# A decoder layer on eight cores: the second core's columns go from one piece to two, on either side of the first core's, and two equal tiles share their instructions

## The chip, the cores and the metric

The kernel runs on all 8 cores of one Trainium2 chip. The input holds four sequences of 4096 positions with 1024 channels; cores 0 and 1 share the first sequence, 2 and 3 the second, and so on. The even core of a pair is the "first core" (role `a` in the code), the odd one the "second core" (role `b`). The pairs do not talk to each other, and neither do the two cores of a pair. The time is that of the slowest core, in microseconds (us) on the device. A TensorE instruction multiplies a 128 x 128 weight block with up to 512 columns; a "column" is one position of the sequence.

## The reference

One layer with two token mixers and a gated channel mixer, cut to what matters:

```
h  = rmsnorm(x)
u_pool, u_rnn, u_gate, g_pool, g_rnn = split(h @ w_in)         # 512 + 4 x 1024 outputs
y_pool = pool_mixer(u_pool) @ w_pool_out                       # trailing windows of 2, 4, 8, 16
v  = conv4(u_rnn)                                              # causal, 4 taps, per channel
r, i = sigmoid(v @ w_a + b_a), sigmoid(v @ w_x + b_x)          # 8 diagonal blocks of 128
a  = exp(-8 * r * softplus(-lam))
hr[t] = a[t] * hr[t-1] + sqrt(1 - a[t]^2) * i[t] * v[t]        # over the whole sequence
y_rnn = (hr * gelu(u_gate)) @ w_rnn_out
x  = x + (sigmoid(g_pool) * y_pool + sigmoid(g_rnn) * y_rnn) @ w_o
x  = x + (silu(rmsnorm(x) @ w_gate) * (rmsnorm(x) @ w_up)) @ w_down   # 2816 inner channels
out = rmsnorm(x)
```

The recurrence `hr` runs over all 4096 positions. A core that gives out columns in the middle or at the end of a sequence must therefore first run the recurrence alone (norm, `u_rnn`, convolution, gates, scan) over every column ahead of them.

## The kernel before, in words

Channels lie on the 128 partitions, positions along the free dimension. Columns 0 to 2239 (`XS = 2240`) are given out by the first core, the other 1856 by the second, which before that runs the recurrence alone over columns 0 to 2239. Such recurrence-only columns are called the prefix. Given-out columns are worked off in two chunks (`own`), and each chunk in tiles of up to 508 columns: 256, 412, 396 and 344, 500, 332 on the first core, 508, 508 and 460, 380 on the second, whose prefix has tiles of 256 and four times 496. A chunk loads all weights of the layer again.

In `chunk`, a given-out column goes through 36 blocks of `w_in` (`wu` recurrence, `wg` its gelu gate, `wq` pool, `wa` and `wb` merge gates), 16 gate blocks `keep_rg`, pool output `keep_wp`, `wr`, `wo`, and then the channel mixer: 22 blocks `wf` (gate and up) and 8 blocks `wz` (down). Counted in matmuls per tile this is 288 + 16 + 32 + 64 + 64 + 352 + 176 = 992; a prefix column needs 64 + 16 = 80. `stat` adds the squares of the channels on TensorE, either with one matmul of a sum made elsewhere or with eight (`"pe"`).

For one head and tile, `rnn_group` has TensorE write `u` into a PSUM bank; ScalarE makes `v` from it (L745) and VectorE adds three taps (L757); GpSimd casts to bf16 (L765); TensorE makes the two gates (L770), ScalarE their tanh (L780) and exp (L788), GpSimd a square (L795), ScalarE a sqrt (L798), VectorE the product and the scan (L815, L828). Instructions from L788 on already cover all tiles of a group.

Nothing of the order is written by hand. `Planner` places every instruction of a role on its engine by a list of keys (the tables in `ROLES`), estimated durations and the space in SBUF and PSUM, and the engines then run that order strictly, with semaphores between them. All weights are issued by GpSimd's DMA queue (`load` with `pool`), all tiles of `x` by SyncE's (`load_tile`). The first instructions (`start`) are common to both roles.

## Time and profile before

| | |
|---|---|
| median of 3 runs (lowest, highest) | 1025.53 us (1024.29, 1219.17) |
| the profiled execution | 1024.35 us |
| its span on the slowest core (core 3, a second core) | 1022.8 us |
| spans of the first cores (0, 2, 4, 6) | 1017.9, 1016.8, 1017.4, 1021.7 us |
| spans of the second cores (1, 3, 5, 7) | 1022.7, 1022.8, 1022.7, 1022.4 us |
| TensorE busy, core 3 / core 2 | 924.4 / 980.4 us |
| mean granted TensorE clock, core 3 / core 2 | 0.951 / 0.986 |

A span runs from the first to the last instruction of a core; the profiled execution's own time is 1.5 us longer than the longest span. PE is TensorE, PEld its weight loads, DVE VectorE, ACT ScalarE, POOL GpSimd, SP SyncE. In a table of stretches the busy time of each engine stands with its number of instructions in brackets, and PEclk is the mean granted clock in that stretch (1.00 is 2.4 GHz, the lower level of 1.2 GHz is 0.50).

### The profile page before, as it was taken

The numbers are of one execution on the slowest core, as the hardware profiler recorded it, in microseconds if no ns is written. First come the engines' busy times: TensorE is split into PE (matmuls) and PEld (weight loads), VectorE is DVE, ScalarE is ACT, GpSimd is POOL, SyncE is SP. The second block draws the span as 40 slices with busy tenths as digits, with TensorE's granted clock in tenths as the row PEclk, the third lists the DMA queues.
The fourth block names the chain that finished last, engine by engine and source line by source line (L and its number), as shares of the span: only waits on it lengthen the run. The fifth ranks groups of instructions, "written<-read, shape, count | busy, mean of one in ns | idle before, by whom it ended". The sixth has DMA issues, their size and how long they took to land.

```text
span 1022.8 us, 13708 instructions; the slowest of 8 cores (1016.8 to 1022.8 us)
## 1 busy us (share of the span) xinstructions
PE 924.4 (90%) x4484; PEld 446.6 (44%) x4484; DVE 591.4 (58%) x798; ACT 556.7 (54%) x804; POOL 336.8 (33%) x347
## 2 busy tenths in 40 slices
PE   2378688698978999999999999999999999999995
PEld 1134233233433444444444444444555555555553
DVE  2179998999999867844253544533644452222235
ACT  2579997989889942548264938611722351111112
POOL 2438593778655641151001122112251211000000
PEclk8579789899989999999999999999999999999998
DMA  8921452003644276768403257255939175910003
GB/s 176 242 69 33 160 93 42 12 1 55 116 82 87 38 192 118 160 98 150 82 8 56 39 80 141 44 101 123 253 69 212 30 129 108 211 41 2 1 1 135
DMA packets 42765, 96.88 MB, mean 95 GB/s; under 512 B 3776, under 2 KB 19264, under 8 KB 42560
## 3 DMA queue, kind: packets, MB, share of 16 engines
q0 software_dynamic: 23904, 63.45, 36.1%
q1 hardware_dynamic: 18784, 32.48, 10.6%
q8 instruction: 40, 0.66, 0.2%
q14 instruction: 37, 0.30, 0.1%
HBM read 151.75 MB, written 7.60 MB: 156 GB/s over the span
## 4 chain that ended last, share of the span: by engine, by line
PE 78%; ACT 9%; issue 5%; POOL 3%; DVE 2%; DMA 2%; ACTq 0%; DVEq 0%; SPq 0%; POOLq 0%
PE bank L705 74%; PE bank L770 2%; PE bank L667 2%; DMA wu<-w_in 2%; ACT th L780 1%; DVE v L757 1%; ACT q L798 1%; POOL sq L638 1%; ACT th L788 1%; ACT v L745 1%; ACT L798 1%; ACT L780 1%; DMA xt<-xT 1%; POOL vb L765 1%; ACT wi L780 0%
## 5 line engine op out<-in xcount | busy, mean ns | idle before, releaser
L705 PE MATMUL bank<-h,wf 128*128 128x508 bf16 (+2 forms) x1408 | 280.7, 358 | 0.0
L705 PEld LDWEIGHTS bank<-h,wf 128*128 128x128 bf16 x1408 | 136.5, 97 | 139.9 <-issue 0.8
L757 DVE SCALAR_TENSOR_TENSOR v<-bank,keep_cst,v 128x496 f32<-128x496 f32 (+3 forms) x200 | 128.8, 683 | 32.4 <-POOL v L754 13.4
L705 PE MATMUL bank<-h,wu 128*128 128x500 bf16 (+4 forms) x576 | 130.1, 381 | 16.3 <-DMA wu<-w_in 11.0
L1084 DVE TENSOR_TENSOR ff<-tf,bank 128x508 bf16<-128x508 f32 (+2 forms) x88 | 55.7, 634 | 147.9 <-PE bank L705 123.5
L705 PE MATMUL bank<-ff,wz 128*128 128x508 bf16 (+2 forms) x704 | 139.5, 359 | 0.0
L1079 ACT ACTIVATE tf<-bank 128x508 f32<-128x508 f32 (+2 forms) x88 | 48.8, 557 | 137.8 <-PE bank L705 134.4
L652 ACT ACTIVATE sq<-x 128x508 f32<-128x508 f32 (+2 forms) x56 | 32.9, 590 | 125.3 <-DVE x L1096 97.4
L705 PEld LDWEIGHTS bank<-ff,wz 128*128 128x128 bf16 x704 | 68.9, 98 | 68.6 <-issue 0.5
L705 PEld LDWEIGHTS bank<-h,wu 128*128 128x128 bf16 x576 | 58.7, 103 | 83.9 <-issue 32.9
L765 POOL CAST vb<-v 128x496 bf16<-128x496 f32 (+3 forms) x68 | 61.1, 905 | 61.4 <-DVE v L757 53.3
L770 PE MATMUL bank<-vb,keep_rg 128*128 128x496 bf16 (+4 forms) x144 | 43.2, 381 | 33.4 <-ACT th L780 10.1
L515 POOL DMA_DIRECT2D wf<-wfi x44 | 23.8, 549 | 147.1 <-PE bank L705 106.0
L795 POOL TENSOR_TENSOR q<-th 128x752 f32<-128x752 f32 (+3 forms) x31 | 56.9, 1843 | 37.8 <-ACT th L788 18.9
L682 DVE SCALAR_TENSOR_TENSOR h<-xt,keep_cst,bank 128x500 bf16<-128x500 f32 (+4 forms) x72 | 45.8, 686 | 30.8 <-ACT bank L674 29.7
L745 ACT ACTIVATE v<-bank,keep_cst 128x496 f32<-128x496 f32 (+3 forms) x72 | 51.7, 732 | 19.1 <-PE bank L705 18.0
L705 PE MATMUL bank<-h,wa 128*128 128x508 bf16 (+2 forms) x256 | 56.6, 367 | 3.0 <-ACT th L780 1.7
L1096 DVE TENSOR_TENSOR x<-bank,x 128x508 f32<-128x508 f32 (+2 forms) x32 | 20.4, 639 | 64.9 <-PE bank L705 64.6
L705 PE MATMUL bank<-h,wg 128*128 128x508 bf16 (+2 forms) x256 | 55.2, 367 | 2.8 <-ACT th L780 1.9
L780 ACT ACTIVATE th<-bank,keep_hb 128x496 f32<-128x496 f32 (+3 forms) x72 | 44.8, 639 | 22.1 <-PE bank L770 21.8
L638 POOL TENSOR_TENSOR sq<-sq,sq 128x1000 f32<-128x1000 f32 (+2 forms) x18 | 41.9, 2330 | 36.9 <-ACT sq L623 30.3
L705 PE MATMUL bank<-h,wb 128*128 128x508 bf16 (+2 forms) x256 | 53.9, 363 | 0.0
(103 smaller groups left out, 1311.7 us busy)
## 6 DMA issues: line engine op xcount, KB each, us to landing
wf<-wfi POOLq DMA_DIRECT2D x44, 512.0 KB, 9.5
wz<-wfo POOLq DMA_DIRECT2D x16, 704.0 KB, 10.1
xt<-xT SPq DMA_DIRECT2D x16, 500.0 KB, 8.6
wu<-w_in POOLq DMA_DIRECT2D x16, 256.0 KB, 13.7
xt<-xT SPq DMA_DIRECT2D x8, 512.0 KB, 21.1
wa<-w_in POOLq DMA_DIRECT2D x16, 256.0 KB, 5.9
wg<-w_in POOLq DMA_DIRECT2D x16, 256.0 KB, 5.4
wb<-w_in POOLq DMA_DIRECT2D x16, 256.0 KB, 5.5
```

The costliest lines, as they stand in the source:

```text
L638: self.ew(adds, 2 * w, key, lambda e, t=t: e.tensor_tensor(out=sq.tensor[:], in0=sq.tensor[:], in1=t.tensor[:], op=ALU.add), [sq, t], [sq] ...
L652: g.op("act", c_act(w), key, lambda e: e.activation(out=s.tensor[:], in_=x2[cc // 2].tensor[:, cc % 2, :], func=AF.Square), rd=[(x2[cc // ...
L682: g.op("dve", c_dve(w) + 0.04, key + 0.1 * kc, lambda e, kc=kc, b=b, o=o, h=h: e.scalar_tensor_tensor(out=o.tensor[:, h, :], in0=b.tensor[ ...
L705: last = e.matmul(p.tensor[:, 0:n], lhsT=wap(kc), rhs=rhs(kc), start=(kc == 0), stop=(kc == K - 1))
L745: g.op("act", c_act(w, 2), k, lambda e, p=p, o=o, w=w: e.activation(out=v.tensor[:, o:o + w], in_=p.tensor[:, HALO:HALO + w], func=AF.Iden ...
L757: g.op("dve", c_dve(w), k, lambda e, p=p, o=o, w=w, s=s: e.scalar_tensor_tensor(out=v.tensor[:, o:o + w], in0=p.tensor[:, HALO - s:HALO - ...
L765: cast = lambda e, vb=vb, o=o, w=w: e.tensor_copy(out=vb.tensor[:], in_=v.tensor[:, o:o + w])
L770: g.op("pe", c_mm(w) + 0.05, k + 1 + 0.3 * q, lambda e, pg=pg, q=q, vb=vb, w=w: e.matmul(pg.tensor[:, 0:w], lhsT=self.rg.tensor[:, q, j, : ...
L780: g.op("act", c_act(w, 1), k + 1 + 0.3 * q, lambda e, pg=pg, out=out, hcol=hcol, w=w: e.activation(out=out(), in_=pg.tensor[:, 0:w], func= ...
L795: g.op("pool", 0.09 + 0.0018 * W, k, lambda e: e.tensor_tensor(out=q2.tensor[:], in0=th.tensor[:], in1=th.tensor[:], op=ALU.mult), rd=allp ...
L1079: g.op("act", c_act(w), kf, lambda e, pg=pg, th=th, w=w: e.activation(out=th.tensor[:], in_=pg.tensor[:, 0:w], func=AF.Silu), rd=[pg], wr= ...
L1084: g.op("dve", c_dve(w), kf, lambda e, pu=pu, th=th, fb=fb, w=w: e.tensor_tensor(out=fb.tensor[:], in0=th.tensor[:], in1=pu.tensor[:, 0:w], ...
```

## The change

The first core now gives out columns 800 to 2923 and the second columns 0 to 799 and 2924 to 4095. Each has a prefix: 800 columns on the first core (tiles 256, 272, 272, ahead of its first chunk, `pre_at=0`), 2124 on the second (424, 424, 416, 428, 432, between its two chunks, `pre_at=1`). The chunks have tiles 508, 508 and 368, 472, 268 on the first core, 256, 272, 272 and 388, 392, 392 on the second. The weights `wu` of the neighbouring chunk are used for the prefix too.

Where two tiles that follow each other have the same width, `rnn_pair` joins them: their `u` and gates go to two neighbouring PSUM banks, and L745, the three L757, L765 and the two L780 are issued once for both. This holds for 272, 272 and 508, 508 on the first core, for 272, 272 and 424, 424 and 392, 392 on the second. A bank pair must be free as a whole (`find_bank`). The gate weights come in four loads, not one. A load of an `x` tile now waits for the weight load that the planner sees end 4 us before it. All tables in `ROLES` are new, so nearly all instructions stand in another order.

```diff
-XS = 2240
+Y0, Y1 = 800, 2924
...
+    def find_bank(self, b, t):
+
+        free = [self.bank_live[i] is None and self.banks[i][0] <= t for i in range(8)]
+        if b.space == "ps2":
+            c = [(max(self.banks[i][0], self.banks[i + 1][0]), i) for i in range(0, 8, 2) if free[i] and free[i + 1]]
+        else:
+            c = [(self.bank_live[i ^ 1] is None, self.banks[i][0], i) for i in range(8) if free[i]]
+        return min(c)[-1] if c else None
...
+        weights = sorted([o for o in self.order["pool"] if o.nbytes], key=lambda o: o.end)
+        for o in self.order["sp"][sum(h.eng == "sp" for h in self.head):]:
+            if o.nbytes and o.tag != "out":
+                begin = o.end - self.prm["dma_lat"] - o.nbytes / self.prm["dma_rate"]
+                t = [x for x in weights if x.end <= begin - 4.0 and x.start < o.start]
+                if t:
+                    o.deps.append(t[-1])
...
+    def rnn_pair(self, j, tiles, wu, key, toff, v, th, wi, cast, off, part):
+        w = tiles[0][1]
+        two = lambda b: b.tensor[:, off:off + 2 * w].rearrange("p (t w) -> p t w", t=2)
+        p = self.banks("ps_u")
...
+        for s in (1, 2, 3):
+            g.op("dve", c_dve(2 * w) + 0.05, k, lambda e, s=s: e.scalar_tensor_tensor(
+                out=two(v), in0=p.tensor[:, :, HALO - s:HALO - s + w],
+                scalar=cst.tensor[:, C_CW + 8 * (3 - s) + j:C_CW + 8 * (3 - s) + j + 1], in1=two(v),
+                op0=ALU.mult, op1=ALU.add), rd=pk + [cst] + vk, wr=vk, tag="cv")
...
+        for ci, widths in enumerate(own):
+            if ci == at:
+                pre, wus, col = self.prefix(col, wus)
+            col, wus = self.chunk(ci, widths, prm["keys"][ci], pre if ci == at else [], wus if ci == at else None, col, ci + 1 == at)
...
-        groups=[], own=[[256, 412, 396], [344, 500, 332]], wp=344.8, window2=183.19,
+        prefix=[256, 272, 272], groups=[1, 2], own=[[508, 508], [368, 472, 268]], wp=268.52, window2=1485.95,
...
-        prefix=[256, 496, 496, 496, 496], groups=[2, 2, 1], own=[[508, 508], [460, 380]], wp=261.84, window2=107.54,
+        prefix=[424, 424, 416, 428, 432], groups=[2, 2, 1], own=[[256, 272, 272], [388, 392, 392]], wp=116.07, window2=8149.02,
```

How the instructions move is shown at three places. In these rows `x2` means the same instruction twice in a row, and `waits d_pool7` names a semaphore of a weight load on GpSimd's queue. The first place is SyncE's queue on the first core, just after the common start; before, it holds the `x` tiles of 416 and 400 columns:

```order
L515 DMA xt_70<-xT 128x2x416
L515 DMA xt_71<-xT 128x2x416
L515 DMA xt_72<-xT 128x2x416
L515 DMA xt_73<-xT 128x2x416
L515 DMA xt_83<-xT 128x2x400
L515 DMA xt_84<-xT 128x2x400
L515 DMA xt_85<-xT 128x2x400
L515 DMA xt_86<-xT 128x2x400
```

and now the second prefix tile (276 with its 4 columns of overlap) and the first chunk's two tiles:

```order
L535 DMA xt_87<-xT 128x2x276 [waits d_pool3]
L535 DMA xt_88<-xT 128x2x276 [waits d_pool4]
L535 DMA xt_89<-xT 128x2x276
L535 DMA xt_90<-xT 128x2x276 [waits d_pool5]
L535 DMA xt_186<-xT 128x2x512 [waits d_pool6]
L535 DMA xt_187<-xT 128x2x512 [waits d_pool7]
L535 DMA xt_188<-xT 128x2x512 [waits d_pool8]
L535 DMA xt_189<-xT 128x2x512 [waits d_pool9]
L535 DMA xt_199<-xT 128x2x512 [waits d_pool10]
L535 DMA xt_200<-xT 128x2x512 [waits s_pe]
L535 DMA xt_201<-xT 128x2x512 [waits d_pool11]
L535 DMA xt_202<-xT 128x2x512 [waits d_pool12,s_dve]
```

The tiles were issued at once; now nearly each waits for one more weight block to land, and there are sixteen of them instead of eight.

The second place is TensorE on the second core, after the first heads of its first tile (`h` the normalised input, `acc` and `sq` sums of squares). Before, recurrence only:

```order
L667 MATMUL bank<-acc_1042,keep_ones_48 128x500
L667 MATMUL bank<-sq_1235,keep_ones_48 128x512
L667 MATMUL bank<-acc_1084,keep_ones_48 128x500
L705 MATMUL bank<-h_1044,wu_59 128x500 x2
L705 MATMUL bank<-h_1045,wu_59 128x500 x2
L705 MATMUL bank<-h_1046,wu_59 128x500 x2
L705 MATMUL bank<-h_1047,wu_59 128x500 x2
L705 MATMUL bank<-h_1044,wu_60 128x500 x2
L705 MATMUL bank<-h_1045,wu_60 128x500 x2
L705 MATMUL bank<-h_1046,wu_60 128x500 x2
L705 MATMUL bank<-h_1047,wu_60 128x500 x2
```

and now:

```order
L729 MATMUL bank<-h_1034,wg_1086 128x256 x2
L729 MATMUL bank<-h_1035,wg_1086 128x256 x2
L729 MATMUL bank<-h_1036,wg_1086 128x256 x2
L729 MATMUL bank<-h_1037,wg_1086 128x256 x2
L729 MATMUL bank<-h_1047,wu_1071 128x276 x2
L729 MATMUL bank<-h_1048,wu_1071 128x276 x2
L729 MATMUL bank<-h_1049,wu_1071 128x276 x2
L729 MATMUL bank<-h_1050,wu_1071 128x276 x2
L729 MATMUL bank<-h_1047,wg_1086 128x272 x2
L729 MATMUL bank<-h_1048,wg_1086 128x272 x2
L729 MATMUL bank<-h_1049,wg_1086 128x272 x2
L729 MATMUL bank<-h_1050,wg_1086 128x272 x2
```

The prefix was all that TensorE had there; now blocks of `wg` (and soon `wb`, `wq`, `wa`) of the first chunk stand between those of `wu`.

The third place is TensorE on the second core in the channel mixer of its first chunk. Before, `wf` follows `wf`:

```order
L667 MATMUL bank<-acc_1427,keep_ones_48 128x508
L705 MATMUL bank<-h_1450,wf_1524 128x508 x2
L705 MATMUL bank<-h_1451,wf_1524 128x508 x2
L705 MATMUL bank<-h_1452,wf_1524 128x508 x2
L705 MATMUL bank<-h_1453,wf_1524 128x508 x2
L705 MATMUL bank<-h_1450,wf_1469 128x508 x2
L705 MATMUL bank<-h_1451,wf_1469 128x508 x2
```

and now:

```order
L729 MATMUL bank<-h_1299,wf_1374 128x256 x2
L729 MATMUL bank<-h_1300,wf_1374 128x256 x2
L729 MATMUL bank<-h_1510,wu_57 128x428 x2
L729 MATMUL bank<-h_1511,wu_57 128x428 x2
L729 MATMUL bank<-h_1512,wu_57 128x428 x2
L729 MATMUL bank<-h_1513,wu_57 128x428 x2
L691 MATMUL bank<-acc_1550,keep_ones_48 128x432
L729 MATMUL bank<-h_1524,wu_57 128x428 x2
L729 MATMUL bank<-h_1525,wu_57 128x428 x2
L729 MATMUL bank<-h_1526,wu_57 128x428 x2
L729 MATMUL bank<-h_1527,wu_57 128x428 x2
L729 MATMUL bank<-h_1307,wf_1360 128x272 x2
```

The whole prefix (`wu` with 420 to 436 columns and the gates) has moved into and behind this stage, between the `wf` blocks of 256 and 272 columns.

## Rows read from the trace of the kernel before

**Rows 1.** Span and mean granted TensorE clock, core by core.

```profile
core 2: 1016.8 us, clock 0.986
core 3: 1022.8 us, clock 0.951
```

**Rows 2.** Chain that ended last, by engine: core 3, then core 2.

```profile
PE 78%; ACT 9%; issue 5%; POOL 3%; DVE 2%; DMA 2%; ACTq 0%; DVEq 0%; SPq 0%; POOLq 0%
...
PE 92%; DMA 2%; DVE 2%; issue 2%; ACT 1%; POOL 0%; SPq 0%; DVEq 0%; ACTq 0%; POOLq 0%
```

**Rows 3.** Busy times by stretch, core 3; the first line names the columns.

```profile
core 3: us, PE busy (x) PEld busy (x) DVE busy (x) ACT busy (x) POOL busy (x), PEclk, DMA share, GB/s
0.00:75.00 75.00, 34.51 (x113) 17.30 (x114) 26.91 (x54) 37.04 (x53) 26.24 (x30) 0.70 0.70 166
75.00:426.00 351.00, 303.63 (x1318) 130.72 (x1317) 315.94 (x359) 277.39 (x393) 209.54 (x170) 0.93 0.41 84
426.00:1000.00 574.00, 574.00 (x2985) 291.57 (x2984) 235.08 (x363) 238.91 (x355) 101.02 (x148) 1.00 0.48 90
1000.00:1023.00 23.00, 12.23 (x73) 6.99 (x71) 13.43 (x24) 3.40 (x7) 0.00 (x0) 0.82 0.43 150
```

**Rows 4.** The same for core 2, first its first 75 us.

```profile
0.00:75.00 75.00, 52.85 (x252) 31.87 (x253) 34.03 (x72) 40.72 (x70) 21.22 (x43) 0.89 0.89 169
...
0.00:243.00 243.00, 218.65 (x1336) 138.47 (x1338) 159.75 (x233) 143.91 (x256) 100.04 (x122) 0.96 0.59 115
243.00:1000.00 757.00, 757.00 (x4675) 457.30 (x4673) 361.08 (x569) 300.97 (x490) 114.60 (x158) 1.00 0.42 83
1000.00:1017.00 17.00, 4.74 (x30) 2.82 (x28) 5.87 (x12) 1.95 (x4) 0.00 (x0) 0.77 0.25 84
```

**Rows 5.** Timeline (start, us, engine): first up-and-gate matmuls, core 2, then core 3.

```profile
243.22 1.91 PE L705 MATMUL bank<-h,wf 128*128 128x256 bf16 x16
...
425.83 5.32 PE L705 MATMUL bank<-h,wf 128*128 128x508 bf16 x24
```

**Rows 6.** Waits of TensorE on core 3: us in total, times, longest.

```profile
PE bank L705 <- DMA wu<-w_in: 11.0, 2, 6.2
...
PE bank L770 <- DVE v L757: 8.5, 5, 4.2
```

**Rows 7.** Matmuls of core 2 by form: count, busy us, mean ns.

```profile
L705 PE MATMUL bank<-h,wf 128*128 128x500 bf16 x352 | 77.8, 373 | 0.0
...
L705 PE MATMUL bank<-h,wf 128*128 128x256 bf16 x352 | 41.3, 272 | 0.0
...
L667 PE MATMUL bank<-sq,keep_ones 128*128 128x416 f32 x16 | 6.2, 522 | 2.0 <-ACT sq L623 2.0
```

**Rows 8.** The statistics matmuls of core 3 by form.

```profile
L667 PE MATMUL bank<-sq,keep_ones 128*128 128x512 f32 x32 | 16.6, 627 | 7.6 <-ACT sq L623 7.5
...
L667 PE MATMUL bank<-sq,keep_ones 128*128 128x260 f32 x16 | 5.3, 505 | 7.9 <-ACT sq L623 7.9
```

**Rows 9.** VectorE on core 3 by form.

```profile
L757 DVE SCALAR_TENSOR_TENSOR v<-bank,keep_cst,v 128x508 f32<-128x508 f32 x48 | 33.0, 734 | 1.4 <-ACT v L745 0.8
...
L1084 DVE TENSOR_TENSOR ff<-tf,bank 128x380 bf16<-128x380 f32 x22 | 12.1, 550 | 39.9 <-PE bank L705 38.4 <-ACT sq L652 1.5
...
L757 DVE SCALAR_TENSOR_TENSOR v<-bank,keep_cst,v 128x256 f32<-128x256 f32 x24 | 11.1, 475 | 12.7 <-ACT v L745 6.3 <-ACT ab L582 5.6
```

**Rows 10.** ScalarE on core 3 by form.

```profile
L798 ACT ACT_TABLE_LOAD x27 | 34.6, 1283 | 1.6 <-POOL q L795 1.1
...
L1079 ACT ACTIVATE tf<-bank 128x380 f32<-128x380 f32 x22 | 10.7, 487 | 45.9 <-PE bank L705 45.9
```

**Rows 11.** Timeline of ScalarE on core 3 around one table load.

```profile
28.71 1.28 ACT L780 ACT_TABLE_LOAD   x1
30.00 0.47 ACT L780 ACTIVATE th<-bank,keep_hb 128x256 f32<-128x256 f32 x1
```

**Rows 12.** Timeline of core 3: the last writes of x.

```profile
1015.67 4.25 DVE L682 SCALAR_TENSOR_TENSOR x<-x,keep_cst,bank 128x380 f32<-128x380 f32 x8 [2.38 <-ACT bank L674]
```

More of the change, by code:

```diff
@@ L164, in can_alloc @@
                 continue
-            if b.space == "ps":
-                if not any(self.bank_live[i] is None and self.banks[i][0] <= t for i in range(8)):
+            if b.space != "sb":
+                if self.find_bank(b, t) is None:
                     return False
@@ L169, in can_alloc @@
                 n += b.nbytes
-        if room and any(b.space == "ps" and b.left is not None for b in o.bufs):
+        if room and any(b.space != "sb" and b.left is not None for b in o.bufs):
             room = 0
@@ L737, in rnn_group @@
         off = 0
+        joined = 0
         for i, (h, w, part) in enumerate(tiles):
+            if joined:
+                joined = 0
+                continue
+            if i + 1 < len(tiles) and tiles[i + 1][1] == w and not (ps or on[2] or on[5]):
+                self.rnn_pair(j, tiles[i:i + 2], wu, key + toff * i, toff, v, th, wi, kk_vb, off, i)
+                joined = 1
+                off += 2 * w
+                continue
             k = key + toff * i
@@ L962, in chunk @@
+        i = 0
+        for gi, n in enumerate(prm["groups"]):
+            base, step, toff = P["rnn"][gi]
+            self.rnn_groups(P["bat"], [(
+                j, [(h, w, None) for h, w in pre[i:i + n]], wus[j], base + step * j + P["off"][gi][j], toff, first and gi == 0, None,
+                self.places(P, j), gi == len(prm["groups"]) - 1) for j in range(8)])
+            i += n
+        return pre, wus, col
+    def chunk(self, ci, widths, kk, pre, wus, col, parted):
         g, dr, prm = self.g, self.dr, self.prm
@@ L979, in chunk @@
         tw = list(zip(hs, widths))
-        first = self.role == "a" and ci == 0
+        first = col == 0
         G = []
```

201 lines of the change are left out of this document (117 added, 84 removed).

## Prediction

> **What bounds the kernel now.** I read the spans first: second and first cores end close together, at 1022.8 and 1016.8 us, but with different clocks [rows 1]. The chain that ended last says why: TensorE is 78% of it on core 3 and 92% on core 2 [rows 2]. So a first core is a TensorE queue with a late start, and a second core is something else in front of one. The stretches show where. Core 2 has TensorE busy for all of 243 to 1000 us at full clock [rows 4]. Core 3 reaches that state only at 426 us; from 75 to 426 us TensorE works 303.6 of 351 us at a mean clock of 0.93 while VectorE is busy 315.9 us [rows 3]: there the recurrence of 2240 prefix columns plus the first chunk keeps VectorE (90%) and ScalarE (79%) as the limit, and TensorE goes idle and, when idle, slow.
>
> I split each span into **work** (TensorE's busy time times its granted clock, what it would take at 2.4 GHz) and **loss** (the rest). Core 3: 34.5 x 0.70 + 303.6 x 0.93 + 574.0 + 12.2 x 0.82 = 890.6 of work, 132.2 of loss: 51 before 75 us, 69 up to 426, 13 in the tail [rows 3]. Core 2: 218.7 x 0.96 + 757.0 + 4.7 x 0.77 = 970.5 of work, 46.3 of loss: 33 up to its first `wf` matmul at 243 us and 13 in the tail [rows 4, 5]. A clock averaged over a stretch is not quite that of its busy time, so these are good to some 3 us.
>
> **The change part by part.** *Columns.* A given-out column is 992 matmul columns and a prefix column 80. First core: 2240 x 992 = 2,222,080 becomes 2124 x 992 + 800 x 80 = 2,171,008, or 51,072 fewer. Second core: 1856 x 992 + 2240 x 80 = 2,020,352 becomes 1972 x 992 + 2124 x 80 = 2,126,144, or 105,792 more. The price is the slope between `wf` matmuls of 500 and 256 columns, 77.8/352 = 221.0 ns and 41.3/352 = 117.3 ns [rows 7]: 0.425 ns a column. That is -21.7 us and +45.0 us, on the path everywhere.
>
> *Narrow tiles.* The same rows leave 8.5 ns fixed per matmul; the whole of core 2 leaves less (2,222,080 x 0.425 = 944.4, three statistics tiles of about 6.2 [rows 7], so 7.5 us over 5952 matmuls, 1.3 ns). I take 3 ns, nearer to the second since overlapping rows count twice. The first core goes from 5952 to 5 x 992 + 3 x 80 = 5200 matmuls, -2 us; the second from 4368 to 6 x 992 + 5 x 80 = 6352, +6 (3 to 17) us.
>
> *Statistics.* The first core adds squares on TensorE for two tiles of 508 instead of 412 and 396: 16.6 [rows 8] for 2 x 6.2 [rows 7], +4 us. The second does it for 272, 272 instead of 508, 508: 2 x 5.5, by the 260 row, for 16.6 [rows 8], -6 us.
>
> So the work is 970.5 - 21.7 - 2 + 4 = 951 us on the first core and 890.6 + 45 + 6 - 6 = 936 us on the second. Evenly shared; what decides is the loss.
>
> *First core, up to its first `wf`.* Now 800 prefix columns stand with 1016 given-out ones. Prices per column come from the stretches. Core 2 up to 243 us, 1064 columns: VectorE 159.8/1064 = 150 ns, ScalarE 143.9/1064 = 135 ns, TensorE work 209.9/1064 = 197 ns [rows 4]. Core 3 up to 426 us less 1016 such columns, over 2240: VectorE (342.9 - 152.4)/2240 = 85 ns, ScalarE (314.4 - 137.2)/2240 = 79 ns, TensorE (306.6 - 200.2)/2240 = 47 ns [rows 3]. The first core now needs VectorE 800 x 85 + 1016 x 150 = 220 us, ScalarE 200 us, TensorE 238 us. *Joining* takes from this: a tap costs 734 ns at 508 and 475 ns at 256 columns [rows 9], so 1.03 ns a column and 212 ns fixed; 16 joined pairs x 3 taps x 0.212 = 10 us less on VectorE (0 if an instruction over two banks pays twice), about as much on ScalarE. VectorE 210, TensorE 238: both near. At core 2's pace for TensorE (209.9 in 243, 86%) the first `wf` comes at 275 us, at core 3's pace for VectorE (342.9 in 426, 80%) at 261 us. Two near limits wait for each other, so I take 278: a loss of 40 us where core 2 had 33. Ends: 30 (better filled than core 2, since TensorE may now draw on more of the chunk) and 62 (first `wf` at 300). The new waits of SyncE lie in this stretch: what queues behind a waiting load is only the next `x` tile, and weights land ahead of them; TensorE waited 11.0 us for `wu` on core 3 before [rows 6], part of which this order gives back. They are inside the 40. GpSimd, with 100.0/1064 = 94 ns and (235.8 - 95.5)/2240 = 63 ns a column [rows 3, 4], needs 146 us and eight squares that move to it, and is no limit; that the gate weights come in four loads moves no work.
>
> *Second core.* Its start is now that of core 2, 800 columns instead of 1064 with the same mix: loss 32. Then the prefix runs beside the channel mixer of chunk one: TensorE 2124 x 47 + 800 x 528 x 0.425 = 279 us; VectorE 2124 x 85 plus 46 passes of `ff`'s 12.1/22/380 = 1.45 ns [rows 9] over 800 columns, less 5 for joining, 229 us (82%); ScalarE 2124 x 79 plus 30 passes of 1.28 ns [rows 10] over 800 columns = 199, plus 20 more table loads (counted in the orders: 101 before, 121 now) at 1.283 us [rows 10], 225 us (81%). Core 2 at 76% VectorE lost next to nothing after its first 75 us; core 3 at 112% (315.9 on 282.4) lost 69. I take 14 us (5 to 40). After 426 us nothing was lost on core 3, and the second chunk is no denser.
>
> *Tail.* The last norm, 4.3 us of VectorE, and the write [rows 12] stay: 13 us on both.
>
> **Sum.** First core 951 + 40 + 13 = 1004 us; second 936 + 32 + 14 + 13 = 995 us. The run lies 1.5 us above the longest span and the median 1.2 us above the profiled run: 1004 + 2.7 = **1007 us**, 1.8% less. What a measurement of this kernel can tell from no change is about 2%, that is 1005.0 us, so the forecast sits at the edge.
>
> **Rivals.** (1) *The first core starts as well as core 2 did*: loss 30, span 994, second core below it at about 990: 997 us. For it: TensorE has blocks of `wg` and `wb` to fill with. Against: these need the tiles of 508 columns landed and normalised, which come behind three prefix tiles, and core 3, which began with a prefix, lost 51 of its first 75 us [rows 3].
> (2) *The second core's middle binds*: VectorE and ScalarE above 80% beside an ordered TensorE queue. Loss 40 there gives 936 + 32 + 40 + 13 = 1021, 1024 us.
> (3) *Joining saves nothing* because two banks cost as two instructions: VectorE back at 220 us, `wf` near 284, 1013 us.
> (4) *Bank pairs stall TensorE*, the case on the other side. A joined head holds two of eight banks until ScalarE (848 x 1.28 ns [rows 10] = 1.1 us) and three taps (0.212 + 848 x 1.03 ns [rows 9] = 1.1 us each) are through, 4.4 us, and its gates take two more pairs. The second core has 24 such heads beside `wf`, which itself needs two banks a tile. Before, TensorE waited only 8.5 us for taps [rows 6]. If every head stalls TensorE for its whole 4.4 us, 24 x 4.4 = 106 us come on top: 995 + 106 + 2.7 = 1104 us. It decides from 48 us on (995 + 48 + 2.7 = 1046, 2% over the median), that is from 11 of the 24 heads.
> (5) *Table loads cost more than their row.* The new order has 49 changes of table between the first and last silu of the second core's first chunk. If something behind each load held ScalarE for as long again, 49 x 1.283 = 63 us [rows 10] would make it 288 us; at the 79% that ScalarE reached beside TensorE on core 3 that takes 365 us, 86 more than TensorE needs: 936 + 32 + 86 + 13 + 2.7 = 1070 us. Against it: the activation behind a load begins 0.01 us after its end [rows 11].
> The Trainium skill (ScalarE: Activation LUTs, What ACT_TABLE_LOAD costs) states such a thing: a change of table set takes 2.66 us, a load of 1.28 us and a drain of 1.38 us. By that the 49 changes would add 68 us, and the sum would be 1076 us, an estimate from that page; the row's load agrees with it, the row behind the load shows no drain.
>
> **How the numbers follow.** The forecast (998 to 1017) 0.52; (1) 0.18; (2) 0.13; (3) 0.10; (4) 0.05; (5) 0.02. Two fifths of the forecast lie below 1005.0: faster by over 2% is 0.18 + 0.21 + 0.02 = 0.41. Slower by over 2% is (4) and (5): 0.07. Within 2%: 0.52. The range of 8 in 10 takes in (1) and most of (2), and leaves (4), (5) and the ends: 994 to 1026.
>
> **What would show it.** First cores: TensorE busy near 958, first `wf` at 270 to 285 us, full from there. Second cores: mean clock up from 0.951 to about 0.98, TensorE busy near 945, PEclk near 1.00 from 100 us on, and idle of a few us, put down to ScalarE or VectorE, between 215 and 480 us. VectorE's joined tap of 1016 columns at about 1.26 us says joining saves. If a second core is the slowest by over 10 us, my loss for its middle is wrong; if first `wf` on a first core comes after 300 us, the start is; if TensorE waits for L757 or L780 in total above 40 us, it is (4).

## The result and the profile after

The changed kernel takes 1035.45 us (median of 4 runs, 1034.02 to 1038.89) beside 1025.19 us for the kernel before: ratio 1.0106, interval 1.0089 to 1.0123. It is 1.1% slower, with an interval clear of 1; the forecast was 1007 us, range 994 to 1026. Ratios and intervals leave out runs in which the cores of one die had a lower granted clock and took some per cent longer, such as the 1219.17 us among the runs of the kernel before.

Which cores end last has turned over. Spans and clocks of the changed kernel:

```profile
core 2: 1028.2 us, clock 0.977
core 3: 1026.4 us, clock 0.979
...
core 6: 1034.3 us, clock 0.975
```

In [rows 1] the second core had the lower clock and ended last; now both kinds have about 0.98, and in each pair of neighbours the first core ends later. The chain that ended last, now on core 6, by engine and then by line:

```profile
PE 89%; DMA 4%; ACT 2%; DVE 2%; issue 2%; POOL 1%; SPq 0%; POOLq 0%; ACTq 0%; DVEq 0%
PE bank L729 85%; DMA xt<-xT 3%; PE bank L691 2%; DMA wu<-w_in 1%; PE bank L803 1%; DVE h L706 1%; PE bank L903 1%; ACT wi L906 0%; DVE x L706 0%; ACT L906 0%; POOL q L855 0%; DVE acc L679 0%; ACT th L906 0%; ACT v L885 0%; POOL sq L644 0%
```

It is the TensorE queue with a late start that [rows 2] showed for a first core. How late, the stretches of core 6 say, cut at its first `wf` matmul (299.0 us; the columns are those of [rows 3]):

```profile
0.00:75.00 75.00, 44.34 (x175) 25.82 (x176) 34.78 (x69) 39.85 (x63) 42.99 (x53) 0.77 0.75 158
75.00:125.00 50.00, 40.52 (x213) 21.49 (x214) 42.10 (x57) 44.94 (x65) 27.96 (x32) 0.93 0.25 43
125.00:299.00 174.00, 168.92 (x807) 76.29 (x811) 135.23 (x127) 105.03 (x158) 85.78 (x75) 1.00 0.45 85
299.00:1000.00 701.00, 699.45 (x3967) 385.45 (x3968) 341.38 (x515) 267.08 (x427) 101.66 (x144) 1.00 0.45 89
1000.00:1034.00 34.00, 20.29 (x155) 15.04 (x153) 15.14 (x32) 7.05 (x13) 0.00 (x0) 0.84 0.30 92
```

and the same core before the change, whose first `wf` came at 247.3 us (core 2's of [rows 5] at 243.2):

```profile
0.00:75.00 75.00, 46.80 (x217) 28.15 (x218) 28.56 (x66) 35.06 (x58) 19.11 (x41) 0.86 0.90 169
75.00:125.00 50.00, 47.85 (x317) 30.42 (x316) 41.17 (x52) 43.91 (x79) 20.40 (x19) 1.00 0.11 27
```

With work and loss as in the prediction (stretch minus busy time times clock), core 6 now loses 40.9 + 12.3 + 5.1 = 58.3 us before its first `wf`, 1.5 us from there to 1000 us, and 17.3 in the tail; before it lost 34.8 + 2.2 = 36.9 up to `wf`. Its work is 34.1 + 37.7 + 168.9 + 699.5 + 17.0 = 957.2 us. The first `wf` of cores 0, 2, 4 and 6 comes at 294.8, 292.2, 299.0 and 299.0 us, and in the same stretches they lose 54.8, 51.7, 58.0 and 58.3 us up to it; before the change it was 32.8, 31.6, 32.7 and 36.9. The means of the four, 55.7 and 33.5, are used below beside core 6, since one core in one execution moves by several us (core 6's span was 1029.0 to 1037.3 us in the four runs).

The stretches of core 3, a second core, whose first `wf` now comes at 216.3 us (the cut is 3 us ahead of it):

```profile
0.00:75.00 75.00, 51.84 (x318) 38.41 (x318) 40.24 (x80) 41.14 (x77) 21.51 (x41) 0.91 0.83 148
75.00:213.00 138.00, 129.85 (x1105) 107.73 (x1105) 87.55 (x149) 88.69 (x163) 50.19 (x63) 0.99 0.63 135
213.00:375.00 162.00, 155.26 (x1198) 116.41 (x1197) 120.70 (x180) 138.96 (x189) 83.61 (x67) 1.00 0.40 79
375.00:450.00 75.00, 59.95 (x372) 37.42 (x371) 60.60 (x85) 64.36 (x88) 39.22 (x38) 0.89 0.29 53
450.00:1000.00 550.00, 546.16 (x3417) 330.84 (x3415) 304.47 (x429) 251.20 (x400) 155.02 (x170) 1.00 0.44 87
1000.00:1026.00 26.00, 13.77 (x80) 7.68 (x78) 9.14 (x17) 3.20 (x6) 0.00 (x0) 0.83 0.22 62
```

Against [rows 3] the slow stretch from 75 to 426 us is gone, as forecast, and its 69 us of loss with it. In its place stand 27.8 + 9.4 = 37 us up to the cut, 6.7 + 21.6 = 28 beside the channel mixer, 4 behind it and 15 in the tail, 84 in all, on 942 us of work.

Joining did what it says. VectorE's taps (L890 joined, L790 single) and ScalarE's scaling and tanh on core 6, by form:

```profile
L890 DVE SCALAR_TENSOR_TENSOR v<-bank,keep_cst,v 128x1016 f32<-128x1016 f32 x24 | 29.7, 1267 | 5.3 <-ACT v L885 2.1 <-ACT keep_hst L865 1.6 <-ACT pb L954 1.4
L890 DVE SCALAR_TENSOR_TENSOR v<-bank,keep_cst,v 128x544 f32<-128x544 f32 x24 | 17.7, 776 | 4.8 <-ACT v L885 4.4
...
L885 ACT ACTIVATE v<-bank,keep_cst 128x1016 f32<-128x1016 f32 x8 | 9.4, 1194 | 4.3 <-PE bank L729 4.3
```

1267 ns stands in place of twice the 734 of [rows 9]; joining saves what the prediction took it to save.

Where the first core's start goes, the chain on core 6 shows (start us, us, what; the pieces of its first 84 us that matter):

```profile
2.06 5.92 DMA xt<-xT
...
10.81 10.87 DMA wu<-w_in
...
21.75 0.37 SPq L535
...
22.17 21.77 DMA xt<-xT
...
49.52 1.90 POOL sq L644
...
51.56 5.46 PE bank L691 x6
...
83.88 5.06 PE bank L729 x15
```

A `wu` block lands at 21.7 us; only then does SyncE, which now waits for it, issue the next `x` tile, and that takes 21.8 us to land, at 43.9. Statistics, the second prefix tile's heads and their recurrence follow, and the first block of a given-out tile (512 columns with its overlap) runs at 83.9 us, on the four first cores at 77.5 to 84.1 us. On cores 0 and 2 the load that the `x` tile waits for is one of the four of the gate weights (landed at 22.5 and 30.5 us). Before the change the first core's second tile had its first block at 49.4 to 55.0 us.

### The profile page after: what moved, and what is told of

It is laid out like the page before. It is cut to its first block, busy times and chain, and to the rows that moved or that the text cites. A ratio compares the mean times of both kernels' runs of the same rounds, so it can differ in the third digit from the quotient of the medians.

```text
span 1034.3 us, 15156 instructions; the slowest of 8 cores (1020.0 to 1034.3 us)
## 1 busy us (share of the span) xinstructions
PE 973.5 (94%) x5311; PEld 524.1 (51%) x5318; DVE 568.6 (55%) x797; ACT 463.9 (45%) x724; POOL 258.4 (25%) x303
## 4 chain that ended last, share of the span: by engine, by line
PE 89%; DMA 4%; ACT 2%; DVE 2%; issue 2%; POOL 1%; SPq 0%; POOLq 0%; ACTq 0%; DVEq 0%
PE bank L729 85%; DMA xt<-xT 3%; PE bank L691 2%; DMA wu<-w_in 1%; PE bank L803 1%; DVE h L706 1%; PE bank L903 1%; ACT wi L906 0%; DVE x L706 0%; ACT L906 0%; POOL q L855 0%; DVE acc L679 0%; ACT th L906 0%; ACT v L885 0%; POOL sq L644 0%
## 5 line engine op out<-in xcount | busy, mean ns | idle before, releaser
L729 PE MATMUL bank<-h,wf 128*128 128x508 bf16 (+3 forms) x1760 | 322.5, 342 | 2.3 <-DVE h L706 1.5
L1167 DVE TENSOR_TENSOR ff<-tf,bank 128x508 bf16<-128x508 f32 (+3 forms) x110 | 65.3, 596 | 204.3 <-PE bank L729 190.3
L729 PE MATMUL bank<-ff,wz 128*128 128x508 bf16 (+3 forms) x880 | 160.7, 343 | 0.0
L1162 ACT ACTIVATE tf<-bank 128x508 f32<-128x508 f32 (+3 forms) x110 | 57.5, 523 | 199.1 <-PE bank L729 198.2
L729 PE MATMUL bank<-h,wu 128*128 128x276 bf16 (+5 forms) x506 | 91.2, 333 | 10.2 <-DVE sp L613 4.7
L729 PEld LDWEIGHTS bank<-h,wu 128*128 128x128 bf16 x512 | 51.9, 102 | 46.9 <-issue 15.2
L828 POOL TENSOR_TENSOR q<-th 128x256 f32<-128x256 f32 (+3 forms) x32 | 51.8, 1627 | 49.9 <-ACT th L821 32.8
L729 PE MATMUL bank<-h,wb 128*128 128x508 bf16 (+3 forms) x320 | 63.2, 349 | 0.2
L729 PE MATMUL bank<-h,wg 128*128 128x508 bf16 (+3 forms) x320 | 61.5, 345 | 1.4 <-ACT keep_wp L634 0.9
L729 PE MATMUL bank<-h,wa 128*128 128x508 bf16 (+3 forms) x320 | 62.5, 343 | 0.2 <-DVE tp L1101 0.2
L790 DVE SCALAR_TENSOR_TENSOR v<-bank,keep_cst,v 128x368 f32<-128x368 f32 (+3 forms) x96 | 50.9, 565 | 18.7 <-ACT v L778 17.0
L679 DVE TENSOR_TENSOR acc<-acc,sq 128x508 f32<-128x508 f32 (+3 forms) x70 | 43.6, 624 | 28.1 <-ACT sq L676 26.4
L729 PE MATMUL bank<-mx,wo 128*128 128x508 bf16 (+3 forms) x320 | 58.7, 343 | 0.1
L729 PE MATMUL bank<-gl,wr 128*128 128x508 bf16 (+3 forms) x320 | 58.7, 343 | 0.0
L890 DVE SCALAR_TENSOR_TENSOR v<-bank,keep_cst,v 128x544 f32<-128x544 f32 (+1 forms) x48 | 47.4, 1021 | 10.1 <-ACT v L885 6.5
```

Source lines behind the costliest of these rows:

```text
L679: self.ew(eng, w, key, lambda e: e.tensor_tensor(out=acc.tensor[:], in0=acc.tensor[:], in1=s.tensor[:], op=ALU.add), [acc, s], [acc], tag ...
L729: last = e.matmul(p.tensor[:, 0:n] if half is None else p.tensor[:, half, 0:n], lhsT=wap(kc), rhs=rhs(kc), start=(kc == 0), stop=(kc == K ...
L790: g.op("dve", c_dve(w) + 0.045, k, lambda e, p=p, o=o, w=w, s=s: e.scalar_tensor_tensor(out=v.tensor[:, o:o + w], in0=p.tensor[:, HALO - s ...
L828: g.op("pool", 0.09 + 0.0018 * W, k, lambda e: e.tensor_tensor(out=q2.tensor[:], in0=th.tensor[:], in1=th.tensor[:], op=ALU.mult), rd=allp ...
L890: g.op("dve", c_dve(2 * w) + 0.05, k, lambda e, s=s: e.scalar_tensor_tensor(out=two(v), in0=p.tensor[:, :, HALO - s:HALO - s + w], scalar= ...
L1162: g.op("act", c_act(w), kf, lambda e, pg=pg, th=th, w=w: e.activation(out=th.tensor[:], in_=pg.tensor[:, 0:w], func=AF.Silu), rd=[pg], wr= ...
```

## The experiments

The theories by their letters: **S**, the new waits of SyncE delay the first core's `x` tiles; **R**, the recurrence of its prefix holds it up; **B**, its given-out tiles come too late, behind the prefix and behind loads that land later than the order assumes. Others stand in words. "Mean loss" is the mean of the four first cores' loss up to their first `wf`, 55.7 us in the changed kernel. Unless something else is said, a kernel is the changed one with the edit shown and its order unchanged; ratios are against the kernel before, and the changed kernel's is 1.0106.

**1. Without SyncE's new waits.**

```diff
...
-                t = [x for x in weights if x.end <= begin - 4.0 and x.start < o.start]
-                if t:
-                    o.deps.append(t[-1])
```

> The changed kernel with the new waits of SyncE taken out: its x loads no longer wait for weight loads that stand ahead of them; every engine's order is the same. Theory S (the first core starts late because the 508-column x tiles are issued only at 25 to 44 us, behind those waits, so that TensorE has nothing but the narrow prefix until about 57 us): first wf matmul on core 6 comes at 287 to 293 us where it came at 299, first cores 6 to 12 us shorter, median 1024 to 1030. Theory R (the recurrence of 800 columns keeps VectorE and ScalarE as the limit until about 150 us, whenever x lands): first wf at 297 to 301, median 1033 to 1037. Third, the x loads then crowd out the weights on the DMA engines, which were full from 15 to 45 us: first wf later than 301, median above 1037.

1028.97 us, ratio 1.0043 (1.0030 to 1.0057): 6.5 us less. First `wf` on cores 0, 2, 4, 6 at 291.1, 292.7, 294.9, 294.4; core 6's loss up to there 52.6, the mean loss 51.9. Core 6's chain shows what is late instead:

```profile
10.61 15.78 DMA wu<-w_in
...
26.53 5.37 PE bank L722 x24
...
47.34 5.31 PE bank L684 x6
...
79.17 5.29 PE bank L722 x16
```

The `x` tile no longer queues, `wu` now lands 4.7 us later (26.4 against 21.7), and the first given-out block still waits until 79 us (75.0 to 79.9 on the four). The waits did what they were put in for: with them TensorE waits 1.5 us for `wu` on core 6 in its first 125 us, without them 12.0. They cost more at the `x` tiles. S holds for 6 of the 21 us by which core 6's start got worse, and for 4 of 22 in the mean.

**2. The joined tiles issued apart** (each joined instruction split in two, bank pairs kept).

```diff
+        each = lambda f: [f(i) for i in range(2)][-1]
...
-                out=two(v), in0=p.tensor[:, :, HALO - s:HALO - s + w],
+                out=two(v)[:, i], in0=p.tensor[:, i, HALO - s:HALO - s + w],
```

> The changed kernel in the same order and with the same bank pairs, but each joined tap, scaling and tanh is issued as two instructions, one for each bank. If joining saves what the rows show (201 ns a tap of 1016 columns, 368 ns a scaling, 275 ns a tanh), a first core gets 16 x (3 x 0.2 + 0.37 + 2 x 0.28) = 24 us more, 10 of VectorE and 15 of ScalarE, before its first wf, and a second core 24 such pairs more than that in its own first half. Theory R: at least half of the first core's 24 us shows, median 1044 to 1060. Theory S: engines have room, at most 5 us show, median 1034 to 1041. Rival J (the pairs themselves stall TensorE, and one instruction over two banks holds them longer): the time falls, below 1033.

1041.82 us, 1.0165 (1.0140 to 1.0190): by the ratios 6 us more, between what R (at least half of 24 us) and its rival (at most 5) expected. Joining is a gain of some 6 us here, so it does not tie TensorE up on balance. The bank pairs were kept, so what they cost alone is not measured.

**3. and 4. A short recurrence in the prefix**, in the first core (3) and in the second (4). Taps, exp, sqrt, products and scan of a prefix column's group cover 16 columns; the other columns of the recurrence are left out. The diff is that of 4; in 3 the role is `'a'`.

```diff
+        few = 16 if gel is None and self.role in 'b' else 4096
...
-                out=hid.tensor[:, o:o + w], data0=th.tensor[:, o:o + w], data1=drive(), initial=init(), op0=ALU.mult, op1=ALU.add),
+                out=hid.tensor[:, o:o + min(w, few)], data0=th.tensor[:, o:o + min(w, few)], data1=drive()[:, 0:min(w, few)], initial=init(), op0=ALU.mult, op1=ALU.add),
```

> The changed kernel in the same order; in the first core's prefix the taps, the input gate's product, the scan, the exponential, the square root and their products work on 16 columns of each tile or head only, so the state that the prefix hands on is wrong; scaling, tanh, cast and all matmuls stay whole. That takes some 50 us from VectorE and 20 from ScalarE in the first 150 us of a first core. Theory R: the start's loss falls from 55 us (core 6) to 40 or less, first wf at 284 or before, median 1015 to 1024 (then the second cores, 1020 to 1026 us, end last). Theory S: first wf moves by at most 4 us, median 1030 to 1036.

1033.55 us, 1.0095 (1.0075 to 1.0114), not separable from the changed kernel's ratio; first `wf` at 294.0, 291.8, 296.8, 290.7: 0.4 to 2.2 us earlier on three cores and 8.3 on core 6. VectorE falls from 42.1 to 23.1 us between 75 and 125 us on core 6, and the stretch still loses 9.3 us of the 12.3. The mean loss is 53.4, 2.3 less. R expected a first `wf` at 284 us or before and a median below 1024: it falls as the main cause.

> The same shortening of the recurrence in the second core's prefix alone (its state is wrong too), same order. If the recurrence is what stops TensorE there at 375 to 430 us, the second cores' spans fall by 18 to 30 us, to 995 to 1006, their first wz comes as much earlier, and the first cores stay at 1028 to 1035, so that the run's time stays within 3 us of 1035. If table loads and the order bind and not the length of the instructions, the second cores fall by less than 10 us. If the two kinds of cores disturb each other over memory, the first cores move by over 3 us too.

One execution, 1036.27 us. The second cores end at 1019.3, 1016.2, 1011.1 and 1007.9 us, 1 to 16 earlier, three of them between what the two theories expected (18 to 30, under 10). The first cores, whose program is unchanged, are where they were: first `wf` at 294.5, 293.8, 299.8 and 298.3, mean loss 55.6, which also shows how well the mean repeats. Core 3 from 375 to 450 us:

```profile
375.00:450.00 75.00, 62.51 (x414) 41.32 (x413) 22.41 (x83) 55.98 (x94) 32.86 (x46) 0.91 0.38 81
```

VectorE has 22.4 us of work instead of 60.6, and 18.1 of 21.6 us of loss stay (16.9 to 18.1 of 20.7 to 21.7 on the four second cores): there too the length of the recurrence is not what TensorE waits for.

**5. Half of GpSimd's squares** (on 1; the first core's first two given-out tiles use half of them twice, the other half is left out).

```diff
+        n = 1 if adds == "pe" and on == "pool" and self.role == "a" else 2
...
+                    out=t.tensor[:, 0:n], in0=b.tensor[:, 0:n], in1=b.tensor[:, 0:n], op=ALU.mult),
```

> As e1_no_sp_waits (SyncE's new waits taken out), and the squares of the first core's first two own tiles on GpSimd take one of the two halves of each x tile (0.95 us where it was 1.9, eight times); TensorE sums that half twice, so the norm of those 1016 columns leaves out half the channels. Same order. Theory G (after the waits are gone GpSimd, busy 20.6 of 25 us from 50 to 75, is what keeps the first 508-column block until 80 us): first wf on core 6 at 289 to 292 us where it was 294.4, median 1024 to 1027. Theory D (the x tiles still land too late for that): first wf within 1.5 us of 294.4, median 1027.5 to 1030.

1031.47 us, 1.0041 (1.0024 to 1.0058), as 1; first `wf` 291.7 to 295.2, first given-out block at 77.6 to 79.5 us. GpSimd's squares are not the limit.

**6. Three loads of `wb` and `wg` later** (on 1; moved on the first core's GpSimd queue behind the third square).

```diff
+        at = [o for o in q if o.tag == "n1sq"][2]
+        late = [o for o in q if o.tag in ("wb", "wg") and o.start < at.start]
...
```

> As e1_no_sp_waits, and three weight loads of the first core (two wb, one wg; 768 KB of the 8 MB moved by 60 us) that are issued at 20 to 23 us and first read at 84 us or later are issued only behind the second square of the first own tile, at about 48 us. All else in the same order. Theory D (the DMA engines, full from 15 to 45 us, set the start): what is left lands about 4 us earlier, TensorE's two waits for wu (12.0 us on core 6) fall by 3 to 5 us, first wf at 289 to 292, median 1024 to 1027. Theory G: first wf within 1.5 us, median 1027.5 to 1030.

1029.97 us, 1.0040 (1.0024 to 1.0055), as 1; TensorE waits 11.9 us for `wu`, as in 1 (12.0). These three loads don't hold `wu` up.

**7. Sqrt replaced by Identity** (the root is left out; ScalarE loads 76 tables instead of 122 on core 3, 62 instead of 86 on core 6).

```diff
-        sr = g.op("act", c_act(W, 1), k + 2, lambda e: e.activation(out=q2.tensor[:], in_=q2.tensor[:], func=AF.Sqrt, scale=-0.25,
+        sr = g.op("act", c_act(W, 1), k + 2, lambda e: e.activation(out=q2.tensor[:], in_=q2.tensor[:], func=AF.Identity, scale=-0.25,
```

> The changed kernel, same order, with the square root of the recurrence's gain left out (ScalarE scales and adds, which needs no table), on all cores. That takes away the 16 table loads in front of L831 on a first core and 30 on a second, and about as many again to come back, 1.283 us each: 20 to 40 us of ScalarE on a first core, 38 to 75 on a second. Theory T (table loads are why ScalarE binds): TensorE's loss at 375 to 450 us on core 3, 20.6 us by its busy time and clock, falls under 8 us and second cores come to 1005 to 1014; on the first cores the loss at 75 to 125 us (12 us on core 6) falls under 6, first wf at 291 to 295, median 1026 to 1031. If the loads lie beside other waits: second cores above 1017, first cores within 2 us of the changed kernel.

1034.54 us, 1.0091 (1.0043 to 1.0139). Core 3 from 375 to 450 us:

```profile
375.00:450.00 75.00, 62.15 (x415) 41.02 (x413) 61.70 (x88) 58.74 (x88) 49.64 (x46) 0.93 0.39 81
```

17.2 us of loss remain of 21.6, nearly what 4 left by the opposite cut; second cores end at 1006 to 1020 us. On the first cores the loss between 75 and 125 us falls to 7.8 to 9.3 us (from 10.4 to 12.3), the first `wf` comes at 292.6, 292.0, 296.6 and 296.0, the mean loss is 53.6. T expected under 8 us in the one stretch and under 6 in the other: it falls as the main cause, and the loads are a small part of both.

**8. Second cores idle** behind their first loads (their half of the output is left out).

```diff
-                emit(e, name, plans["b"], n)
+                emit(e, name, plans["b"], n, n)
...
```

> The changed kernel with the second cores doing nothing behind their first loads (their half of the output is left out); the first cores run what they ran. If the loads of the eight cores hold each other up, the first cores' bytes land sooner: from 25 to 45 us more than the 173 to 300 GB/s of core 6, the first wf at 285 to 293 on cores 4 and 6 (299.0) and the gap of these to cores 0 and 2 closes. If a core's own 16 DMA engines are the limit (they showed a busy share of 1.05 there), the rates and the first wf stay within 2 us.

First `wf` at 289.2, 292.5, 293.0, 289.8: 5.6, 0, 6.0 and 9.2 us earlier; the mean loss is 50.9. Transfers of core 6 from 25 to 45 us (last two columns: share and GB/s), first the changed kernel

```profile
25.00:35.00 10.00, 2.67 (x15) 1.47 (x12) 3.86 (x9) 3.99 (x6) 3.82 (x5) 0.67 1.06 173
35.00:45.00 10.00, 5.61 (x22) 3.12 (x22) 1.02 (x2) 6.24 (x13) 6.14 (x8) 0.58 1.07 300
```

then with idle second cores:

```profile
25.00:35.00 10.00, 5.23 (x22) 2.69 (x21) 3.83 (x8) 9.05 (x18) 9.51 (x14) 0.63 1.11 249
35.00:45.00 10.00, 6.16 (x15) 2.84 (x13) 6.86 (x12) 9.25 (x15) 9.08 (x9) 0.52 1.07 353
```

The queues are equally full, and bring more in. So part of the spread between first cores is the second cores' loading, but with it gone the first `wf` is still at 289 to 293. Core 0 ended last in all three executions (1074.5 to 1081.6 us), with 66 us of loss between its first `wf` and 1000 us in the profiled one; why is open, so only the start is read.

**9. First core planned anew** (on 1; loads before 60 us counted at 190 GB/s, its table searched again; the second core's order is unchanged).

```diff
-                    dma_free = s + o.nbytes / prm["dma_rate"]
+                    dma_free = s + o.nbytes / (prm["early"] if s < 60.0 else prm["dma_rate"])
```

> SyncE's new waits out, and the first cores' order planned anew: the planner counts loads that begin in the first 60 us at 190 GB/s (core 6 moved 171 to 300 GB/s there) where the changed kernel counts 265, and the numbers of the first core's table were searched again for that; the second cores keep their order. Theory S (the start is lost since the order expects x and weights sooner than they land, and lies elsewhere in the order): the first cores lose 8 to 15 us less than in e1_no_sp_waits, spans 1010 to 1019, the second cores (1018 to 1023) end last, median 1020 to 1026. Theory B (the bytes themselves bound the start: a prefix gives TensorE 80 matmul columns for each x column where own columns give 992, in any order): first cores stay at 1022 to 1030, median 1025 to 1031.

1025.97 us, 0.9998 (0.9986 to 1.0009): level with the kernel before, and the fastest order found for this change. But the start did not gain by it: core 6 loses 40.4 + 10.5 + 2.1 = 53 us up to its first `wf` at 290.8, as much as in 1; the mean loss is 50.7 against 51.9. Theory B's expectation held (first cores at 1022 to 1024 us). The first `wf` comes earlier than in 1 because TensorE has less work ahead of it (34.6 + 39.5 + 163.9 = 238 against 242).

**10. Only the first prefix tile in the first core** (on 9; columns 256 to 799 are left out of its prefix).

```diff
-        return pre, wus, col
+        return pre, wus, 800 if self.role == "a" else col
...
-        prefix=[256, 272, 272], groups=[1, 2],
+        prefix=[256], groups=[1],
```

> As e9_first_replanned, with the first core's prefix cut to its first tile: columns 256 to 799 are left out of its recurrence (a wrong state is handed on) and neither loaded nor normalised; own columns and tables stay, the order follows from them. The work falls by 544 x 80 x 0.425 ns and two statistics, 21 us. Theory B (in front of its own columns a prefix gives TensorE too little work for the bytes and the recurrence that it brings): the loss in front of the first wf falls as well, from 53 us on core 6 to 33 to 42, near what the first cores of the kernel before had, first cores at 985 to 994. If the loss comes from elsewhere (the order, joining, the shared memory): it stays at 48 to 55 us, first cores at 998 to 1006. The second cores stay at 1016 to 1024 in both.

One execution. First cores end at 995.1, 993.7, 995.7 and 1000.9 us, first `wf` at 257.0, 257.5, 257.0 and 263.3; the second cores (to 1024.5) set the end, at 1026.06. The first given-out block on core 6 and its stretches:

```profile
55.76 1.87 PE L722 MATMUL bank<-h,wb 128*128 128x508 bf16 x8 [0.26 <-DVE h L699]
```

```profile
0.00:75.00 75.00, 45.27 (x157) 22.72 (x159) 26.95 (x58) 25.20 (x40) 33.06 (x47) 0.82 0.84 159
75.00:125.00 50.00, 49.81 (x240) 22.84 (x241) 36.47 (x30) 43.80 (x69) 23.54 (x21) 1.00 0.33 74
125.00:263.00 138.00, 131.24 (x615) 58.38 (x618) 101.93 (x104) 78.86 (x118) 64.48 (x59) 0.99 0.43 73
```

The given-out block comes 23 to 28 us earlier (51.1 to 55.8 us on the four, where the second tile's was before the change), and the loss between 75 and 125 us, 8 us or more on core 6 in each kernel with the whole prefix, is 0.2. In all 39.5, 41.3, 39.3 and 46.2 us are lost up to `wf` on cores 0, 2, 4 and 6, against 50.3, 50.2, 49.4 and 53.0 in 9. Core 6, by which the expectations were written, lies between B's and its rival's: the two further prefix tiles cost 7 to 11 us of waiting beside their work.

**11. and 12. The old share-out with everything else** (columns 0 to 2239 and the rest; joined tiles, bank pairs, four gate loads, no new SyncE waits, both tables searched anew); 12 issues the joined tiles apart, as 2.

```diff
-Y0, Y1 = 800, 2924
+Y0, Y1 = 0, 2240
```

> The columns shared out as before the change (first core 0 to 2239 with no prefix, second core the rest behind a prefix of 2240), with the change's other parts: tiles of one width joined (24 pairs on a second core, none on a first), bank pairs, gate weights in four loads; SyncE's new waits are out, and both tables were searched again for this. If the new share-out is what costs, and joining what gains: the second cores, held by VectorE (90%) and ScalarE (79%) from 75 to 426 us before, lose 24 x 0.6 us of VectorE and 24 x 0.9 us of ScalarE there, first wf at 405 to 420, spans 1006 to 1018; the first cores, with a loss of 32 to 37 us in front of their first wf as before, 1014 to 1022; median 1015 to 1023, below both kernels. If joining gains nothing where the recurrence binds: second cores 1020 to 1026, median 1022 to 1028.

> As e11_old_split, in the same order, with each joined tap, scaling and tanh issued as two instructions. If joining is worth its rows where VectorE and ScalarE bind, the second cores end 10 to 22 us later than in e11_old_split and end last, median 1022 to 1040; in the changed kernel the same edit cost 6.4 us. If their waits hide it: at most 5 us. The first cores, which have no pairs, stay within 3 us.

1044.52 us, 1.0187 (1.0171 to 1.0203), and 1048.38 us, 1.0222 (1.0206 to 1.0239). The expectation of 11 missed on both kinds of cores; in 12 its branch for a small gain holds, 3.9 us for joining. The second cores end at 1042 to 1044 us in 11. They have 16 joined heads (24 taps of 992 and 24 of 1016 columns), not the 24 of the expectation. Core 3:

```profile
0.00:75.00 75.00, 29.44 (x94) 14.71 (x94) 25.95 (x54) 34.03 (x46) 35.20 (x37) 0.70 0.87 221
75.00:440.00 365.00, 304.84 (x1306) 129.82 (x1306) 316.53 (x308) 280.51 (x358) 203.87 (x158) 0.91 0.34 67
```

With joined taps it loses 54 and 88 us where [rows 3] lost 51 and 69. VectorE's busy time there did not fall (316.5 us, in [rows 3] 315.9), and why the order that the search found waits longer was not settled. So 11 does not say what the share-out alone is worth; it says that joining alone does not mend a second core that begins with its prefix. It says one thing more: its first cores, with no prefix, no new waits and the old tiles, lose 40.5 to 43.1 us in their first 75, where those of the kernel before lost 28.0 to 34.8. Core 6:

```profile
0.00:75.00 75.00, 43.13 (x207) 26.36 (x208) 31.75 (x64) 35.80 (x61) 13.82 (x30) 0.80 0.76 139
```

Beside the order, only the gate weights in four loads and what the second cores load meanwhile differ from the kernel before there. So some 10 us of loss in a first core's start come without any prefix; that it is the new order is likely, but not shown.

## Why the prediction was wrong, by its steps

**The step that failed** is "Two near limits wait for each other, so I take 278: a loss of 40 us where core 2 had 33". It measured 58 on core 6 and 52 on core 2, with `wf` at 292 to 299 us, inside the stated end of 62 but taken far from it. The sign that I had set for this, a first `wf` after 300 us, stood too late to show it. The TensorE work in it was right: 34.1 + 37.7 + 168.9 = 240.7 against 238. The limits that I weighed, VectorE beside TensorE, were the wrong ones: cutting the recurrence (3) or GpSimd's squares (5) leaves the start within 3 us of where it was, in the mean of the four first cores. What was priced far too low is that TensorE has no given-out block to fill with until the 508-column tiles are there behind three prefix tiles: its first such block runs at 77 to 84 us, and at 51 to 56 with the two further prefix tiles gone (10). I named that against rival (1) and gave it 7 us. The steps on core 6 are

| up to the first `wf` | core 6 loss, us | added | mean loss, us | added |
|---|---|---|---|---|
| before | 36.9 | | 33.5 | |
| one prefix tile in front, two own tiles of 508, all orders new (10) | 46.2 | 9.3 | 41.6 | 8.1 |
| all three prefix tiles (1; 53.0 and 50.7 in 9) | 52.6 | 6.4 | 51.9 | 10.3 |
| new waits of SyncE (changed kernel) | 58.3 | 5.7 | 55.7 | 3.8 |

The last two steps are shown by taking the thing out, the last by 1, the other by 10 against 9. The first is not apportioned: it holds the first prefix tile, the wider tiles and the new order together, and in 11 the first cores lose as much more in their first 75 us without any prefix.

Three errors of size share it. The base should have been core 6, the later of the first cores (36.9), not core 2 (33): 4 us. The sentence that SyncE's waits "are inside the 40" was wrong: what queued behind a waiting load was not only one `x` tile but, through it, the statistics and everything that hangs on it; 6 us of loss on core 6, 6.5 of the run (1). What stands in front, the prefix and the order with it, costs 15 to 16 rather than 7; 7 to 11 of it are the two further prefix tiles.

**The clock, the work, the tail.** First core: work 957 against 951, tail 17 against 13 (the last stretch's mean clock makes the split of these two uncertain by some 3 us). With the start that is 6 + 18 + 1.5 + 4 = 30 us, from 1004 to 1034.3. The run lies 1.2 us above the longest span, not 2.7. TensorE was busy 973.5 us on core 6 and 956.8 on core 3, where I had said near 958 and 945; the second cores' mean clock of 0.98 came as forecast.

**The second core** had its place right and its sizes small: work 942 (936), start 37 (32), middle 28 (14, bound 40), behind it 4 (0), tail 15 (13): 1026 where I gave 995. I had taken the middle's loss from the busy shares of VectorE and ScalarE, and that is not borne out: 4 took 38 us of VectorE's work out of the stretch, and 18.1 of 21.6 us of loss stayed. The middle's loss is concentrated in one stretch, and its chain on core 3 shows how:

```profile
404.60 0.69 ACT v L778
...
405.31 1.28 ACT L1162
406.59 0.01 issue
406.60 0.41 ACT tf L1162
...
407.14 0.85 PE bank L803 x2
...
419.91 1.28 ACT L1162
421.19 0.01 issue
421.20 0.41 ACT tf L1162
...
421.75 0.35 PE bank L803
```

The gates (L803) of the prefix wait for a bank that `tf` of the channel mixer must empty, and `tf` stands on ScalarE behind recurrence work and a table load. That wait is 7.2 us in two pieces on core 3, of 15 us that TensorE is idle in the stretch. This is rival (2)'s place, ScalarE and VectorE beside an ordered TensorE queue; with 28 us it stayed under (2)'s 40. It mattered less than the start, but it alone would have kept the kernel from gaining: in 10, with first cores at 995 to 1001 us, the run still takes 1026.

**Rivals.** (1) is out, by the start. (3) is out: 1267 ns, and 6 us in 2. (4) is out: these are TensorE's longest waits on core 3,

```profile
PE bank L691 <- ACT sq L647: 13.2, 4, 7.3
PE bank L803 <- ACT tf L1162: 7.2, 2, 3.8
PE bank L729 <- ACT th L813: 6.4, 8, 2.1
...
PE bank L729 <- DVE v L890: 3.6, 3, 1.8
```

and those for taps (L890) are 3.6 us, against 8.5 in [rows 6]. Its count was wrong as well: 24 joined heads are all that the second core has, and only the 8 of two times 424 columns stand beside the first chunk's `wf` (24 taps of 848 columns between 213 and 436 us), so by its own 4.4 us a head it could have cost 35 us, less than the 48 from which it was to decide. A slower kernel is what came, but not by (4). (5) is out: with 46 fewer table loads on core 3 (7) the stretch keeps 17 of its 21.6 us, and nothing follows a load in the rows above. Of the chance of a gain over 2% (0.18 + 0.21 + 0.02) the last term had no source.
The Trainium skill (ScalarE: Activation LUTs, What ACT_TABLE_LOAD costs) puts a drain of 1.38 us beside the load at each change of set. Here `tf` begins 0.01 us after the load (406.60, 421.20), as in [rows 11], and the load begins 0.02 us after the instruction ahead of it (404.60 + 0.69, 405.31). The measurement decides against the drain at these places.

**What stays open.** Each single cut (3, 7 and 8 against the changed kernel, 5 and 6 against 1) moves the first `wf` by 5 us at most in the mean of the four first cores, perhaps since another link of the same chain then ends last: the loss of core 6 between 75 and 125 us is 12.3 us in the changed kernel and 9.3, 8.2, 10.6, 11.8, 13.5, 11.6 and 10.5 in 3, 7, 8, 1, 5, 6 and 9. That several links stand equally late there is argued from this, not shown link by link. Of the second core's stretch from 375 to 450 us, 17 of 21.6 us outlast either cut (4, 7), and both cuts together were not tried. How the first 8 to 9 us of the table divide between prefix, tiles and order is not known. What the share-out is worth with an equally good order for both is not known (11).
